# Seven products of a slab pair in another order, diagonal copies on ScalarE, first loads on ScalarE's queue, last sums first

## The chip, the cores and the metric

One core of a Trainium2 chip. The metric is the device time of one execution in microseconds (us), as the median of the runs shown; lower is better.

## The reference, cut to what matters

One inference step of a diffusion backbone with a single trunk layer, on 128 context tokens and 512 latent tokens together (640 columns), model width 1024, in float32:

```
h = rms_norm(x, norm_pre[0]) * (1 + sc1) + sh1
x = x + 0.5 * g1 * rms_norm(swiglu(h, ffn_w_in[0], ffn_w_out[0]), norm_post[0])
h = rms_norm(x, norm_pre[1]) * (1 + sc2) + sh2
m, s_f, s_b = mixer(h, ...)        # Fourier mixing and a two-way HGRN2 scan of 4 heads
x = x + g2 * rms_norm(m, norm_post[1])
h = rms_norm(x, norm_pre[2]) * (1 + sc3) + sh3
x = x + 0.5 * g3 * rms_norm(swiglu(h, ffn_w_in[1], ffn_w_out[1]), norm_post[2])
```

where `swiglu(h) = (silu(h @ Wg) * (h @ Wu)) @ Wout` with 2816 hidden columns, and the shifts, scales and gates come from `silu(cond) @ w_mod + b_mod`.

## The kernel before, in words

Every large product is made of three passes over a split of both operands into a high part (a rounding copy, `_hi`, made by ScalarE) and a low part (the remainder, `_lo`, made by GpSimd or VectorE by a subtraction): hi*hi, hi*lo and lo*hi. Weights are streamed as slabs of 128 columns. SyncE loads a slab when `slab_done` says that its buffer is free, ScalarE makes its high part (`next_hi`, L1201 to L1208), GpSimd its low part (L550), TensorE multiplies. Each engine has its program written out by hand, in order, and waits on semaphores, so an instruction behind a waiting one waits too.

**Front.** SyncE issues eight small loads (identity, vectors) and then five tiles of x, two slabs of `w_mod`, three weight slabs and two more slabs of `w_mod` (L413 to L434). TensorE transposes the vectors, runs 52 idle transposes (`keep_busy`), and transposes the five normalized tiles. ScalarE squares and scales the tiles (L1229, L1235). Then come two products with `w_mod` (`early_mod`), whose row ScalarE copies out (`mod_rows`, L1246) before it makes the first high parts; TensorE folds the row; VectorE makes the modulation vectors (L1700, L1710) and the first h (L1717, L1732); `first_slab` (L827) multiplies the first three slabs step by step, as h comes. GpSimd makes the low parts of those slabs in six halves (`FIRST_LO`).

**Heads.** While TensorE runs the four slabs of head h, it also runs the seven levels of the scan of head h-1. At each level VectorE scales queries and keys (`scale_queries` with L1975 to L1992, `scale_keys` L1959 and L1960), ScalarE copies keys (`level_keys`, L1466), and TensorE runs the level's small products (L951). At level 6 VectorE also copies the 32x32 blocks of ATN onto the diagonal of AT (four copies, L1991), between four copies beside the diagonal (L1992). After level 7's keys TensorE transposes the keys (`keys_to_tokens`, L656).

**Seven products.** For 18 of the 22 slab pairs of the second FFN, a gate slab and a value slab are multiplied by Strassen's scheme, with seven products of half size and sums on VectorE. One product (`product`, L1145) is 12 matmuls of 320 columns. Per pair p there are four result banks x, y, z, v, and seven products in this order: (1) x from the gate's first half; (2) y from s2; (3) x again from the gate's second half, added to the bank; (4) y again from the value's first half, added; (5) z from s1; (6) v from the value's second half; (7) z again from s4, added. Before (3), ScalarE has to copy x out to A_P1 (`p1_copied`, L1644). VectorE then makes U2 = P1 + y after (2) (L2261), U3 = P1 + y after (4) (L2269), C22 = U3 + z after (5) (L2274), C21 after (6) (L2281), the first half of the hidden tile (L2284), C12 after (7) (L2223), and the second half (L2228). Between these it makes the sums s1, s2 and a difference (L2190 to L2195) and s4 (L2204) of the next pair, and two low parts of it (`lows`, L2213 and L2216). ScalarE applies SiLU to x (L1648) after (3) and to C12 (`second_gate`, L1633), and makes the high parts of the next pair; GpSimd makes five low parts of it (L559). Each engine does this in a fixed order; ScalarE runs `second_gate` of pair p-1, then the copy of x of pair p, and `second_gate` waits for C12.

**Split of the hidden tiles.** After pair 17 the 22 hidden tiles, held whole in M32, are split: ScalarE makes the high part (`whole_high`, L1335), VectorE the low part (`whole_low`, L2233). The last product, out1A and out1B (L631 to L633), starts when the first two tiles are split and its first slab is ready. ScalarE makes that slab's high part in `after_slab` behind the SiLU of x of pair 17.

**Last sums.** When out1A is done, VectorE adds sums of squares (`y_sum`, L1750) and updates x (`x_add`, L1755 and L1757) for three tiles, one tile after the other, and then makes low parts of out1B's slabs 6, 9 and 12 (`slab_low`, L1793). ScalarE runs `y_std` (L1275) of each tile between the high parts of out1B's slabs.

Of the kernel before, what the change touches and what calls it, by code (L numbers as in the profile page):

```python
# [3 lines left out]
P = 128  # L4
# [125 lines left out]
def hybrid_step_kernel(nc, x_prompt, x_sample, state_hgrn, c, c_ctx, w_mod, b_mod, norm_pre, norm_post,  # L130
# [280 lines left out]
    def _(sp):  # L411

        sp.dma_start(ident[:, :], t_const).then_inc(sem("const_in"), 16)  # L413
        sp.dma_start(rowsA[0:72, :], b_mod.rearrange("l (r q) -> (l r) q", q=P)).then_inc(sem("rows_in"), 16)
        sp.dma_start(rowsA[72:96, :], norm_pre.rearrange("l s (r q) -> (l s r) q", q=P)).then_inc(sem("rows_in"), 16)
        sp.dma_start(rowsA[96:120, :], norm_post.rearrange("l s (r q) -> (l s r) q", q=P)).then_inc(sem("rows_in"), 16)
        sp.dma_start(rowsB[0:4, :], hgrn_gain.rearrange("l (r q) -> (l r) q", q=P)).then_inc(sem("rows_in"), 16)
        sp.dma_start(rowsB[4:20, :], lb_logits.rearrange("l d (r q) -> (l d r) q", q=P)).then_inc(sem("rows_in"), 16)
        sp.dma_start(rowsB[20:28, :], c.rearrange("l (r q) -> (l r) q", q=P)).then_inc(sem("rows_in"), 16)
        sp.dma_start(rowsB[28:36, :], c_ctx.rearrange("(r q) -> r q", q=P)).then_inc(sem("rows_in"), 16)  # L420
# [126 lines left out]
    def _(pool):  # L547
# [5 lines left out]
        for i, half in FIRST_LO:  # L553
            pool.wait_ge(hi_done, i + 1)
            if (i, half) == (2, 0):
                pool.wait_ge(sem("h0_ready"), KT // 2)
            subtract(i, 4 * half, 4 * half + 4).then_inc(sem("first_lo"), 1)
# [3 lines left out]
        def seven_low(p):  # L561
# [31 lines left out]
    def _(pe):  # L593
# [111 lines left out]
        keep_busy(52, PP[3][:, 0, 0:P])  # L705
# [265 lines left out]
        def outputs(hd):  # L971

            pe.wait_ge(sem("sv_done"), hd + 1)
# [182 lines left out]
        for p in range(SEVEN):  # L1156
# [26 lines left out]
            if p > 1:  # L1183
                pe.wait_ge(sem("hid_b"), p - 1)
            product(z, s1, T1).then_inc(sem("product"), 1)
            pe.wait_ge(sem("seven_lo"), 5 * p + 4)
# [11 lines left out]
    def _(act):  # L1198
# [22 lines left out]

        act.wait_ge(sem("const_in"), 16)
# [28 lines left out]

        mod_rows(2, modrow[0])
        next_hi()
# [214 lines left out]

        def load_states(hd):
# [92 lines left out]
        for m, (n, pr) in enumerate(((0, 0), (0, 1), (1, 0))):  # L1562
            level_keys(last, 2 * m + 2)
            level_keys(last, 2 * m + 3)
# [31 lines left out]
        def value_highs(p):  # L1596
# [4 lines left out]
            A(s2[0][:, :, :], s2[2][:, :, :], ACT.Copy).then_inc(sem("seven_hi"), 1)  # L1601
            act.wait_ge(sem("s_made"), 4 * p + 3)
# [735 lines left out]
```

## Time and profile before

| what | value |
|---|---|
| median of 3 runs | 1442.42 us (1439.97 to 1444.91) |
| the profiled execution's own time | 1442.57 us |
| its span, first to last instruction | 1440.0 us |
| TensorE busy (matmul) | 1404.4 us, 98% |
| VectorE busy | 722.6 us, 50% |
| ScalarE busy | 527.9 us, 37% |
| GpSimd busy | 658.7 us, 46% |
| mean granted TensorE clock | 0.996 |

The span is shorter than the execution's time by the 2.57 us that lie around it. TensorE's busy time is that of pipelined matmuls, so it says where TensorE waits, and not that it works at its peak.

### The profile page before, as it was taken

What the parts mean: (1) busy time and instruction counts of PE and PEld (TensorE: products, weight loads), DVE (VectorE), ACT (ScalarE), POOL (GpSimd) and SP (SyncE); (2) the same over time, 40 slices, a digit from 0 to 9 for tenths busy, and PEclk for the clock granted to TensorE, in tenths of its full rate; (3) what the DMA queues carried; (4) which work ended last, traced back from release to release, by engine and by line L of the source; (5) the groups of instructions that cost most, each with busy time, mean ns of one, the idle gap of its engine ahead of it and who ended that gap; (6) DMA issues with size and microseconds to landing.
All of it is one profiled execution on the core that took longest, in us unless ns stands there. A gap on an engine that the chain in (4) does not pass through costs nothing.

```text
span 1440.0 us, 23202 instructions
## 1 busy us (share of the span) xinstructions
PE 1404.4 (98%) x9661; PEld 1294.8 (90%) x9661; DVE 722.6 (50%) x1067; ACT 527.9 (37%) x791; POOL 658.7 (46%) x507
## 2 busy tenths in 40 slices
PE   6999999999999999999999999999999999989998
PEld 5899999999888888998989999989999999978876
DVE  3388888211001431478777312144677777766043
ACT  6312222222334663233434222266344334345233
POOL 0333433344566682323223433543455565558663
PEclk9999999999999999999999999999999999999999
DMA  9766664222545551212112222413122232235465
GB/s 320 267 211 214 203 235 133 67 80 76 174 129 164 175 198 47 61 52 61 51 40 64 74 73 74 146 59 103 45 74 80 82 88 74 74 89 159 132 184 181
DMA packets 215291, 173.32 MB, mean 120 GB/s; under 512 B 6472, under 2 KB 175636, under 8 KB 215060
## 3 DMA queue, kind: packets, MB, share of 16 engines
q1 hardware_dynamic: 212820, 170.78, 37.7%
q8 instruction: 76, 1.25, 0.3%
q10 hardware_dynamic: 2368, 1.07, 0.3%
q14 instruction: 27, 0.22, 0.1%
HBM read 168.65 MB, written 3.17 MB: 119 GB/s over the span
## 4 chain that ended last, share of the span: by engine, by line
PE 82%; DVE 9%; issue 4%; ACT 2%; DMA 1%; SPq 1%; POOL 0%; DVEq 0%; ACTq 0%
PE PP L612 42%; PE PP L631 8%; PE PP L633 8%; PE PP L632 8%; PE PP L1145 7%; DVE W_lo L2216 2%; DVE S_in L2204 2%; PE PP L656 1%; PE PP L827 1%; PE PP L670 1%; PE PP L951 1%; DMA XTOK<-in_x_sample 1%; DVE TT L2223 1%; PE PP L967 1%; DMA W_in<-in_ffn_w_out 1%
## 5 line engine op out<-in xcount | busy, mean ns | idle before, releaser
L550 POOL TENSOR_TENSOR W_lo<-W_in,W_hi 128x512 fp32r<-128x512 f32 (+1 forms) x380 | 481.0, 1291 | 645.7 <-ACT W_hi L1208 639.1
L1208 ACT ACTIVATE W_hi<-W_in 128x1024 fp32r<-128x1024 f32 x181 | 190.9, 1057 | 445.6 <-PE PP L612 262.5
L612 PE MATMUL PP<-Hhi,W_hi 128*128 128x320 f32 (+2 forms) x1216 | 285.9, 313 | 0.0
L612 PE MATMUL PP<-Hlo,W_hi 128*128 128x320 f32 (+2 forms) x1216 | 280.9, 309 | 0.0
L612 PE MATMUL PP<-Hhi,W_lo 128*128 128x320 f32 (+2 forms) x1216 | 280.8, 309 | 0.0
L612 PEld LDWEIGHTS PP<-Hhi,W_hi 128*128 128x128 f32 x1216 | 202.6, 188 | 9.0 <-issue 6.9
L612 PEld LDWEIGHTS PP<-Hhi,W_lo 128*128 128x128 f32 x1216 | 204.4, 188 | 0.0
L612 PEld LDWEIGHTS PP<-Hlo,W_hi 128*128 128x128 f32 x1216 | 204.4, 188 | 0.0
L559 POOL TENSOR_TENSOR W_lo<-W_in,W_hi 128x512 fp32r<-128x512 f32 x54 | 77.7, 1453 | 99.1 <-DVE W_in L2195 93.0
L1877 DVE SCALAR_TENSOR_TENSOR PP<-modl,S,PP 128x512 f32<-128x512 f32 x144 | 95.8, 744 | 0.0
L631 PE MATMUL PP<-W_hi,Mlo 128*128 128x512 f32 x220 | 86.8, 395 | 4.8 <-DVE Mhi L2233 3.2
L631 PE MATMUL PP<-W_hi,Mhi 128*128 128x512 f32 x220 | 86.3, 392 | 0.8 <-POOL W_lo L550 0.3
L633 PE MATMUL PP<-W_hi,Mhi 128*128 128x512 f32 x220 | 86.3, 392 | 0.0
L632 PE MATMUL PP<-W_lo,Mlo 128*128 128x512 f32 x220 | 86.2, 392 | 0.0
L632 PE MATMUL PP<-W_lo,Mhi 128*128 128x512 f32 x220 | 85.7, 389 | 0.0
L633 PE MATMUL PP<-W_hi,Mlo 128*128 128x512 f32 x220 | 85.6, 389 | 0.0
L1793 DVE TENSOR_TENSOR W_lo<-W_in,W_hi 128x1024 fp32r<-128x1024 f32 x13 | 18.8, 1443 | 115.8 <-ACT W_hi L1208 115.8
L1145 PE MATMUL PP<-Hhi,W_hi 128*128 128x320 f32 x216 | 67.9, 315 | 7.6 <-ACT TT L1644 7.6
L1856 DVE TENSOR_TENSOR TT<-TT,PP 128x640 f32<-128x640 f32 x22 | 18.1, 822 | 108.9 <-PE PP L612 106.8
L1145 PE MATMUL PP<-Hlo,W_hi 128*128 128x320 f32 x216 | 66.8, 309 | 0.0
L1145 PE MATMUL PP<-Hhi,W_lo 128*128 128x320 f32 x216 | 66.7, 309 | 0.0
L631 PEld LDWEIGHTS PP<-W_hi,Mlo 128*128 128x128 f32 x220 | 41.6, 189 | 15.2 <-DVE Mhi L2233 3.5
(294 smaller groups left out, 2682.6 us busy)
## 6 DMA issues: line engine op xcount, KB each, us to landing
W_in<-in_ffn_w_out SPq DMA_DIRECT2D x176, 256.0 KB, 3.1
W_in<-in_ffn_w_in SPq DMA_DIRECT2D x83, 512.0 KB, 3.9
modl<-in_w_mod SPq DMA_DIRECT2D x14, 2048.0 KB, 9.2
W_in<-in_w_in SPq DMA_DIRECT2D x32, 512.0 KB, 3.9
modw<-in_w_mod SPq DMA_DIRECT2D x4, 2048.0 KB, 14.2
HL<-g_rows SPq DMA_DIRECT2D x6, 512.0 KB, 5.7
V_in<-in_w_in SPq DMA_DIRECT2D x10, 256.0 KB, 3.6
O_in<-in_w_out SPq DMA_DIRECT2D x10, 256.0 KB, 6.0
```

Source lines behind the costliest of these rows:

```text
L550: return nc.gpsimd.tensor_tensor(lo[:, k0:k1, :], full[:, k0:k1, :], hi[:, k0:k1, :].bitcast(fp32), ALU.subtract)
L559: return nc.gpsimd.tensor_tensor(lo, full, hi.bitcast(fp32), ALU.subtract)
L612: m = mm(out[:, 0:c1 - c0], w[:, k, :], src[:, c0:c1], start=lead and n == 0 and a == 0, stop=tail and n == len(x) - 1 and a == 2)
L631: mm(out, xh, wh, start=lead and kk == 0, stop=False)
L632: mm(out, xh, wl, start=False, stop=False)
L633: m = mm(out, xl, wh, start=False, stop=tail and kk == 1)
L1145: m = mm(out, wk[:, k, :], xk[:, k, :], start=not add and k == 0 and a == 0, stop=k == KH - 1 and a == 2, skip_group_check=add)
L1208: A(W[i][0], W[i][2], ACT.Copy).then_inc(hi_done, 1)
L1793: V.tensor_tensor(lo, full, hi.bitcast(fp32), ALU.subtract).then_inc(sem("lo_dve"), 1)
L1877: m = V.scalar_tensor_tensor(acc if k < KT - 1 else mod_set(i)[cnd][:, :], w, weight, acc, ALU.mult, ALU.add)
L2204: V.tensor_tensor(s4[2][:, :, :], gate[2][:, KH:KT, :], s2[2][:, :, :], ALU.subtract)\
L2216: V.tensor_tensor(lo, full, hi.bitcast(fp32), ALU.subtract).then_inc(sem("seven_lo_dve"), 1)
```

## The change

Five parts. (a) The eight small loads move from SyncE's queue to ScalarE's, ahead of all else there; the copies of the vectors move behind the first two squares; `keep_busy` has 56 transposes in place of 52; the first slab's high part is made ahead of the copy of the modulation row; GpSimd's low part of the second slab waits for the first finished h. (b) ScalarE makes the four diagonal copies of each head, between the key copies of levels 6 and 7. (c) The order of the seven products is x, y, z, y again, x again, v, z again; GpSimd's and ScalarE's parts of the next pair follow that order, s4 is made before U3, and the SiLU of x comes behind the next pair's high parts. (d) In the last pair the first four hidden tiles are split beside the products. (e) The three `y_sum` come first, then `slab_low` and `x_add` in turn.

```diff
@@ SyncE, and at the head of ScalarE's program with act in place of sp
-        sp.dma_start(ident[:, :], t_const).then_inc(sem("const_in"), 16)
-        sp.dma_start(rowsA[0:72, :], b_mod.rearrange(...)).then_inc(sem("rows_in"), 16)
...
@@ GpSimd
-            if (i, half) == (2, 0):
-                pool.wait_ge(sem("h0_ready"), KT // 2)
+            if half == 0 and i:
+                pool.wait_ge(sem("h0_ready"), (1, KT // 2)[i - 1])
...
+            low(*(x[:, :, :] for x in s1)).then_inc(sem("seven_lo"), 1)
+            pool.wait_ge(sem("seven_hi"), 7 * p + 5)
             low(*(x[:, 0:KH, :] for x in value)).then_inc(sem("seven_lo"), 1)
-            pool.wait_ge(sem("seven_hi"), 7 * p + 5)
-            low(*(x[:, :, :] for x in s1)).then_inc(sem("seven_lo"), 1)
@@ TensorE
-        keep_busy(52, PP[3][:, 0, 0:P])
+        keep_busy(56, PP[3][:, 0, 0:P])
...
         def outputs(hd):
+            pe.wait_ge(sem("at_diagonal"), hd + 1)
...
             product(y, s2, T2).then_inc(sem("product"), 1)
-            pe.wait_ge(sem("seven_lo_dve"), 2 * p + 2)
-            pe.wait_ge(sem("p1_copied"), p + 1)
-            product(x, part(gate, KH, KT), b21, True).then_inc(slab_done, 1)
             pe.wait_ge(sem("seven_lo"), 5 * p + 2)
+            if p == 0:
+                pe.wait_ge(sem("t_lo"), 2)
+            if p > 1:
+                pe.wait_ge(sem("hid_b"), p - 1)
+            product(z, s1, T1).then_inc(sem("product"), 1)
+            pe.wait_ge(sem("seven_lo"), 5 * p + 3)
             pe.wait_ge(sem("u2_done"), p + 1)
...
             product(y, part(value, 0, KH), T3, True).then_inc(sem("product"), 1)
-            pe.wait_ge(sem("seven_lo"), 5 * p + 3)
...
-            product(z, s1, T1).then_inc(sem("product"), 1)
+            pe.wait_ge(sem("seven_lo_dve"), 2 * p + 2)
+            pe.wait_ge(sem("p1_copied"), p + 1)
+            product(x, part(gate, KH, KT), b21, True).then_inc(slab_done, 1)
             pe.wait_ge(sem("seven_lo"), 5 * p + 4)
...
             product(v, part(value, KH, KT), T4).then_inc(slab_done, 1)
@@ ScalarE
-        act.wait_ge(sem("vec_T"), 2)
-        A(VA[:, :], PP[2][:, 0, 0:120], ACT.Copy).then_inc(sem("vec_evac"), 1)
-        A(VB[:, :], PP[2][:, 1, 0:36], ACT.Copy).then_inc(sem("vec_evac"), 1)
         for t in range(NCH):
+            if t == 2:
+                act.wait_ge(sem("vec_T"), 2)
+                A(VA[:, :], PP[2][:, 0, 0:120], ACT.Copy).then_inc(sem("vec_evac"), 1)
+                A(VB[:, :], PP[2][:, 1, 0:36], ACT.Copy).then_inc(sem("vec_evac"), 1)
             act.wait_ge(sem(f"x_in{t}"), 16)
...
+        next_hi()
         mod_rows(2, modrow[0])
-        next_hi()
         next_hi()
...
+        def diagonal_blocks(hd):
+            act.wait_ge(sem("at_done"), 7 * hd + 5)
+            if hd:
+                act.wait_ge(sem("o_mm"), hd)
+            tiles = AT[:, :].rearrange("p (a b) -> p a b", a=NCH)
+            for q in range(4):
+                part = slice(32 * q, 32 * q + 32)
+                m = A(tiles[part, :, part], ATN[part, :, :], ACT.Copy)
+            m.then_inc(sem("at_diagonal"), 1)
...
                     level_keys(h - 1, 2 * m + 2)
+                    if m == 2:
+                        diagonal_blocks(h - 1)
                     level_keys(h - 1, 2 * m + 3)
...
             if p + 1 < SEVEN:
                 gate_highs(p + 1)
+                value_highs(p + 1)
+            else:
+                for j in range(EARLY_PAIRS):
+                    whole_high(j)
             act.wait_ge(slab_done, i + 1)
             A(x, x, ACT.Silu).then_inc(sem("gate_a"), 1)
-            if p + 1 < SEVEN:
-                value_highs(p + 1)
...
-        for j in range(EARLY_PAIRS):
-            whole_high(j)
         second_gate(SEVEN - 1)
@@ VectorE
                 for t in GROUP[0]:
                     y_sum(2, t)
+                for t in GROUP[0]:
+                    slab_low("out1B", (6, 9, 12)[t])
                     x_add(2, t)
-                for m in (6, 9, 12):
-                    slab_low("out1B", m)
...
                 for q in range(4):
-                    V.tensor_copy(tiles[part, :, part], ATN[part, :, :])
                     m = V.tensor_copy(tiles[part, :, other], near(pair_of(hd, lev))[part, :, :])
...
                 first_sums(p + 1)
-            dve.wait_ge(sem("product"), 5 * p + 3)
+                last_sum(p + 1)
+            else:
+                whole_low(0)
+            dve.wait_ge(sem("product"), 5 * p + 4)
...
             V.tensor_tensor(A_U3, A_P1, y, ALU.add).then_inc(sem("u3_done"), 1)
-            dve.wait_ge(sem("product"), 5 * p + 4)
...
             V.tensor_tensor(A_C22, A_U3, z, ALU.add).then_inc(sem("c22_done"), 1)
             if p + 1 < SEVEN:
-                last_sum(p + 1)
                 lows(p + 1)
+            else:
+                whole_low(1)
+                whole_low(2)
...
-        for j in range(EARLY_PAIRS):
+        for j in range(3, EARLY_PAIRS):
             whole_low(j)
```

## Rows read from the trace of the kernel before

**Rows 1.** The page's first part: busy us (share of the span), instructions.

```profile
PE 1404.4 (98%) x9661; PEld 1294.8 (90%) x9661; DVE 722.6 (50%) x1067; ACT 527.9 (37%) x791; POOL 658.7 (46%) x507
```

**Rows 2.** Waits of TensorE, whole span: waiting line, releaser, us, times, longest.

```profile
PE PP L1145 <- ACT TT L1644: 7.6, 17, 0.8
...
PE PP L656 <- DVE KD L1960: 3.3, 3, 1.1
PE PP L631 <- DVE Mhi L2233: 3.2, 1, 3.2
```

**Rows 3.** Timeline of TensorE, one slab pair: start us, us, instruction, idle before.

```profile
1098.93 0.39 PE L1145 MATMUL PP<-Hhi,W_hi 128*128 128x320 f32 x1 [0.41 <-ACT TT L1644]
...
1111.17 0.31 PE L1145 MATMUL PP<-T_hi,S_lo 128*128 128x320 f32 x1
1111.89 0.39 PE L1145 MATMUL PP<-Hhi,W_hi 128*128 128x320 f32 x1 [0.41 <-ACT TT L1644]
```

**Rows 4.** Timelines of VectorE and ScalarE in the same pair.

```profile
1111.78 0.49 DVE L2261 TENSOR_TENSOR TT<-TT,PP 128x320 f32<-128x320 f32 x1 [0.86 <-ACT TT L1644]
...
1111.33 0.42 ACT L1644 ACTIVATE TT<-PP 128x320 f32<-128x320 f32 x1
```

**Rows 5.** The page's DMA issues: count, KB each, us to landing.

```profile
W_in<-in_ffn_w_in SPq DMA_DIRECT2D x83, 512.0 KB, 3.9
```

**Rows 6.** Timelines of TensorE, ScalarE and GpSimd around the end of pair 17.

```profile
1280.38 0.50 PE L631 MATMUL PP<-W_hi,Mlo 128*128 128x512 f32 x1 [3.24 <-DVE Mhi L2233]
...
1270.14 0.42 ACT L1648 ACTIVATE PP<-PP 128x320 f32<-128x320 f32 x1 [2.17 <-PE PP L1145]
...
1271.60 2.56 POOL L550 TENSOR_TENSOR W_lo<-W_in,W_hi 128x512 fp32r<-128x512 f32 x2 [6.48 <-ACT W_hi L1208]
```

**Rows 7.** Window around it: us, busy of each engine, granted clock, DMA.

```profile
1268.00:1290.00 22.00, 18.65 (x95) 16.60 (x96) 10.88 (x15) 11.42 (x16) 8.11 (x6) 0.92 0.33 96
```

**Rows 8.** Timeline of one head: VectorE from level 5 to level 7, then ScalarE.

```profile
674.89 0.33 DVE L1986 COPY_PREDICATED ATN<-near_mask,PP 128x160 f32<-128x160 uint8 x1
...
678.01 0.30 DVE L1991 COPY AT<-ATN 32x160 f32<-32x160 f32 x1
...
680.55 0.49 DVE L1959 TENSOR_TENSOR KD<-KD,FD 128x320 f32<-128x320 f32 x1
...
676.36 0.74 ACT L1466 ACTIVATE KX<-KD 128x640 f32<-128x640 f32 x1 [3.58 <-DVE KD L1960]
```

**Rows 9.** Timeline of the front: SyncE's issues, ScalarE, VectorE.

```profile
0.74 0.40 SPq L413 DMA_DIRECT2D ident<-in_t_const  x1
...
3.82 0.36 SPq L421 DMA_DIRECT2D XTOK<-in_x_prompt  x1
...
10.24 14.52 SPq L434 DMA_DIRECT2D W_in<-in_ffn_w_in  x3
...
14.00 1.06 ACT L1229 ACTIVATE YB<-XTOK 128x1024 f32<-128x1024 f32 x1
...
27.66 0.60 ACT L1246 ACTIVATE modrow<-PP 128x512 f32<-128x512 f32 x1 [3.56 <-PE PP L670]
...
28.15 2.00 ACT L1208 ACTIVATE W_hi<-W_in 128x1024 fp32r<-128x1024 f32 x2
...
29.90 1.91 DVE L1710 SCALAR_TENSOR_TENSOR Avec<-MV,VA 128x4 f32<-128x4 f32 x2
...
47.59 0.36 DVE L1710 SCALAR_TENSOR_TENSOR Avec<-MV,VA 128x4 f32<-128x4 f32 x2
```

**Rows 10.** DMA issues from 9.9 to 11 us: count, KB, us from issue to landing.

```profile
W_in<-in_ffn_w_in SPq DMA_DIRECT2D x1, 512.0 KB, 16.4
```

**Rows 11.** Timeline of ScalarE in the heads: two DMA issues on its own queue.

```profile
640.20 0.83 ACTq L1489 DMA_DIRECT2D out<-SO  x2
```

**Rows 12.** Waits of TensorE from 1300 to 1440 us.

```profile
PE PP L631 <- POOL W_lo L550: 1.2, 2, 0.8
PE PP L631 <- DVE W_lo L1793: 0.3, 1, 0.3
```

More of the change, by code:

```diff
@@ L411, in _ @@
     def _(sp):
-        sp.dma_start(ident[:, :], t_const).then_inc(sem("const_in"), 16)
[L414 to L420, printed above, removed]
         sp.dma_start(XTOK[:, 0, :], x_prompt[0]).then_inc(sem("x_in0"), 16)
@@ L1179, in _ @@
             product(y, part(value, 0, KH), T3, True).then_inc(sem("product"), 1)
-            pe.wait_ge(sem("seven_lo"), 5 * p + 3)
+            pe.wait_ge(sem("seven_lo_dve"), 2 * p + 2)
+            pe.wait_ge(sem("p1_copied"), p + 1)
+            product(x, part(gate, KH, KT), b21, True).then_inc(slab_done, 1)
+            pe.wait_ge(sem("seven_lo"), 5 * p + 4)
             if p == 0:
                 pe.wait_ge(sem("t_lo"), 3)
-            if p > 1:
-                pe.wait_ge(sem("hid_b"), p - 1)
-            product(z, s1, T1).then_inc(sem("product"), 1)
-            pe.wait_ge(sem("seven_lo"), 5 * p + 4)
             if p > 1:
@@ L1219, in root_table @@
             A(spare[:, n:n + 1], ident[:, 0:1], ACT.Sqrt)
+        act.dma_start(ident[:, :], t_const).then_inc(sem("const_in"), 16)
+        act.dma_start(rowsA[0:72, :], b_mod.rearrange("l (r q) -> (l r) q", q=P)).then_inc(sem("rows_in"), 16)
+        act.dma_start(rowsA[72:96, :], norm_pre.rearrange("l s (r q) -> (l s r) q", q=P)).then_inc(sem("rows_in"), 16)
+        act.dma_start(rowsA[96:120, :], norm_post.rearrange("l s (r q) -> (l s r) q", q=P)).then_inc(sem("rows_in"), 16)
+        act.dma_start(rowsB[0:4, :], hgrn_gain.rearrange("l (r q) -> (l r) q", q=P)).then_inc(sem("rows_in"), 16)
+        act.dma_start(rowsB[4:20, :], lb_logits.rearrange("l d (r q) -> (l d r) q", q=P)).then_inc(sem("rows_in"), 16)
+        act.dma_start(rowsB[20:28, :], c.rearrange("l (r q) -> (l r) q", q=P)).then_inc(sem("rows_in"), 16)
+        act.dma_start(rowsB[28:36, :], c_ctx.rearrange("(r q) -> r q", q=P)).then_inc(sem("rows_in"), 16)
         act.wait_ge(sem("const_in"), 16)
         root_table(0)
-        act.wait_ge(sem("vec_T"), 2)
-        A(VA[:, :], PP[2][:, 0, 0:120], ACT.Copy).then_inc(sem("vec_evac"), 1)
-        A(VB[:, :], PP[2][:, 1, 0:36], ACT.Copy).then_inc(sem("vec_evac"), 1)
         for t in range(NCH):
+            if t == 2:
+                act.wait_ge(sem("vec_T"), 2)
+                A(VA[:, :], PP[2][:, 0, 0:120], ACT.Copy).then_inc(sem("vec_evac"), 1)
+                A(VB[:, :], PP[2][:, 1, 0:36], ACT.Copy).then_inc(sem("vec_evac"), 1)
             act.wait_ge(sem(f"x_in{t}"), 16)
@@ L1563, in _ @@
             level_keys(last, 2 * m + 2)
+            if m == 2:
+                diagonal_blocks(last)
             level_keys(last, 2 * m + 3)
@@ L1601, in value_highs @@
             A(s2[0][:, :, :], s2[2][:, :, :], ACT.Copy).then_inc(sem("seven_hi"), 1)
+            A(s1[0][:, :, :], s1[2][:, :, :], ACT.Copy).then_inc(sem("seven_hi"), 1)
             act.wait_ge(sem("s_made"), 4 * p + 3)
             A(value[0][:, 0:KH, :], value[2][:, 0:KH, :], ACT.Copy).then_inc(sem("seven_hi"), 1)
-            A(s1[0][:, :, :], s1[2][:, :, :], ACT.Copy).then_inc(sem("seven_hi"), 1)
             act.wait_ge(raw_full[BUF[i + 1]], NEED[i + 1])
@@ L1619, in _ @@
                 if (grp, j) == (1, 0):
-                    for c, (hi, _, whole) in enumerate((T2, T1, T4)):
+                    for hi, _, whole in (T2, T1, T4):
                         act.wait_ge(sem("t_made"), 4)
@@ L2201, in last_sum @@
             if p:
-                dve.wait_ge(sem("product"), 5 * (p - 1) + 4)
+                dve.wait_ge(sem("product"), 5 * (p - 1) + 3)
             dve.wait_ge(sem("s_made"), 4 * p + 2)
```

## The prediction

> **What bounds the kernel now.** I read the page first: TensorE is busy for 98% of the span [rows 1], VectorE for half. So only time in which TensorE stands still can be won, some 36 us in all. The second view is the table of TensorE's waits [rows 2]. The reader sees there that three names carry most of it: 17 waits of the seven products for ScalarE's copy of x, 3 waits in the heads for the keys of level 7, and one wait ahead of the last product. The third view is the timeline of one slab pair [rows 3, 4], where the wait repeats; the fourth and fifth are the timeline and the window around the end of the pairs [rows 6, 7]; then the heads [rows 8], the front [rows 9 to 11] and the waits of the last product [rows 12].
>
> **Part c, the order of the seven products.** Per pair the idle time is read start to start: 0.72 us between the last matmul ahead of the wait and the first behind it, against 0.147 for a running one ((1111.17 - 1098.93) / 83), so 0.57 lost, and the first matmul takes 0.39 in place of 0.31 [rows 3]. That is 0.65 a pair, and 17 pairs wait [rows 2]: 11.0 us. One period is 1111.89 - 1098.93 = 12.96 us, while 84 matmuls by 0.147 need 12.3. Why is it 12.96? It is a loop: product (3) of a pair waits for the copy of x, that for SiLU of C12 on ScalarE, that for C12 on VectorE, which stands behind C21, the two lows and s4, and those behind C22, which needs product (5) of the pair before. So the loop holds three products, (3), (4) and (5), 3 x 12 x 0.147 = 5.3 us, and 12.96 - 5.3 = 7.7 us of VectorE, ScalarE and signalling.
>
> After the change x is added fifth, with two more products ahead of it, so the copy of x is 3.5 us less urgent. What becomes urgent is U2: product (4) still needs it. Product (1) starts at 1111.17 + 0.15 - 3.52 = 1107.80; U2 ended at 1111.78 + 0.49 = 1112.27 [rows 4], 4.5 us later, and the new product (4) starts 3 x 1.76 = 5.3 us after (1). So even if nothing came earlier, U2 would be 0.8 us in time. The new loop holds one product, (4), with U3 behind it: 1.8 + 7.7, without s4 (it now waits for product (3) and goes ahead of U3) and with U2 and U3 at 0.5 each: some 9.5 us, under the 12.3 that TensorE needs. The five highs of the next pair go ahead of SiLU of x; they have no hurry, since x comes two products later. The gate slab's buffer is now freed by the fifth product in place of the third, 3.5 us later; its load takes 3.9 us [rows 5] and the slab is multiplied only two pairs later, 24 us, so ScalarE and VectorE find it some 2 us before they need it. SyncE's queue holds nothing else there. I cost these moves at nothing; without that cover a late load would stall the highs, and TensorE some 4 us after that. I take 11.0; the ends are 5 (U2 late by some 0.3 in each pair) and 11.7 (pair 0 and longer pairs too).
>
> **Part d, the end of the pairs.** TensorE idles 3.24 us [rows 6], and then the granted clock falls: over 22 us it is 0.92 [rows 7], which is 0.08 x 22 = 1.8 us at full speed, the lower level (1.2 GHz) for some 3.5 us. Lost: 5.0. Tiles 0 to 3 are split during pair 17: four highs on ScalarE behind the copy of x, three lows on VectorE behind sums that pair 18 would have needed, so in free time. What is late next is the first slab of the last product: its high part stands behind SiLU of x on ScalarE. Before, SiLU began at 1270.14 and the low part was done at 1271.60 + 2.56 = 1274.16 [rows 6], 4.0 us behind product (3) and its SiLU. SiLU now comes behind the fifth product, and two products, 3.5 us, are left: so 4.0 - 3.5, and 0.2 for the signal to SiLU (an estimate), 0.7 us of idle time remain, up to 1.2 if VectorE's lows slow GpSimd. I assume that so short a wait costs no clock. Gain 5.0 - 1.0 = 4.0, between 2.5 and 4.6.
>
> **Part b, the heads.** Eight copies lie between 678.01 and 680.55 [rows 8], 0.32 each; half of them go, 1.27 us, right ahead of level 7's keys, for which TensorE waits 1.1 us three times, 3.3 in all [rows 2]. ScalarE's four copies can begin when level 5's predicated copy ends, 674.89 + 0.33 = 675.22, in the 3.58 us of idle time before the key copy at 676.36 [rows 8]. The trace shows no such copy on ScalarE: at VectorE's 0.32 four take 1.3 and end at 676.5, 0.1 late; at 0.74, what the whole key copy takes, they end 1.8 late, which would delay the keys of level 7 by 0.6 or so, as VectorE reaches them 1.27 earlier. I take the first, for its size is the nearer. The fourth head waits for nothing there and gains nothing. Gain 3.3, between 1.5 and 3.5.
>
> **Part a, the front.** SyncE issued x's first load at 3.82; now at 0.74: every load behind it, w_mod and weights too, comes 3.1 us earlier, less 0.4 (an estimate) for sharing the engines with 0.16 MB of small loads that used to run alone. ScalarE now issues those: two took 0.83 us [rows 11], so eight take 3.3, until 4.1, and its first square waits for x anyway. What then sets the modulation row is the first slab's load, since its high part now stands ahead of the row's copy: landed at 10.24 + 16.4 = 26.6 before [rows 9, 10], now at 23.9; with 1.0 for the high part (two took 2.00) the row's copy starts at 24.9 in place of 27.66 [rows 9]: 2.8 won. The two Avec instructions took 1.91 us while GpSimd made low parts, and 0.36 in the second round without it [rows 9]. The first low part is now over by then and the second waits: 1.55 won. But that second low part (one half, 1.28, like those of rows 6) starts with the first h, and TensorE has only six matmuls, 0.9 us, of the other slab: 0.4 lost. The four more idle transposes fall into a pause. Sum 3.9, between 0 and 5.
>
> The Trainium skill ("DMA: Bandwidth & Descriptors", section "Issuing engines are not separate DMA queues") says that issuing from a second engine saves only the issuing time, as all loads share the same DMA engines. By that alone the front would win at most those 3.1 us and the whole sum would be 0.8 smaller; the Avec term is no matter of loads, so I keep my sum.
>
> **Part e.** In the last product TensorE waits 1.5 us in three places for low parts of slabs 4 to 6 [rows 12]. ScalarE's high parts stand behind `y_std`, which waits for a `y_sum` that stood behind an `x_add`. With the sums first, slabs 5 and 6 are in time; slab 4's is behind the first sum as before, and its GpSimd half only loses the contention. Gain 1.1, between 0.4 and 2.
>
> **Sum.** 11.0 + 4.0 + 3.3 + 3.9 + 1.1 = 23.3. The profiled execution took 1442.57 us, 0.15 over the median 1442.42, so 1442.57 - 23.3 = 1419.3, and 1419 for the median.
>
> **Rivals.**
> - **The stall moves to U2.** If U2 is late, product (4) waits in each pair. For it: U2 has only 0.8 to 1 us to spare. Against: C12 comes sooner, as it no longer stands behind s4. At 0.3 us a pair 5 to 6 us are lost: 1425.
> - **Small loads land behind x.** The vectors are awaited at the third square. If the small loads queue behind the five tiles, they land with the last of them, at 14.0 - 3.1 = 11 [rows 9]; with transposes and copies three squares of 1.06 and their sums remain, and the row is 1 us later than before in place of 2.8 earlier. The front then wins nothing: 1423. No row shows two queues loaded at once. The Trainium skill (the same page, "Queues, rings and completion order") says that a DMA engine serves the queues in turns, packet by packet; by that the small loads land about as before and this rival falls.
> - **Slower: VectorE's loop becomes the bound.** Place: lows, C21, C12 and U2 of one pair, with GpSimd beside them. The other parts win 12.3 us, so the pairs would have to lose those: 12.3 / 18 = 0.7 a pair above 12.96, a loop of 13.7. That decides if the new loop, some 9.5, grows by more than 4 us, as if both lows took over twice as long. At a loop of 14 it gives 1442.4 + 6 = 1448. Nothing in the trace speaks for it.
> - **Nothing gained.** Every wait is replaced by another just behind it: 1440 to 1442.
>
> **How the numbers follow.** Forecast 0.72, U2 0.10, small loads 0.12, slower 0.02, nothing 0.04. About 0.3%, 4.3 us, is what a measurement here can tell from no change. The forecast's own range is 1414 to 1424, from the ends of its terms; with the first two rivals and a scatter of 2.5 us in the runs shown the range is 1414 to 1426. Faster by over 0.3%: 0.94; within: 0.04; slower: 0.02.
>
> **What would show it.** Right: no waits of L1145 for ScalarE and a period of 12.3 us; the first matmul of the last product within 1.2 us of the last of pair 17, and a full granted clock behind it; no wait for the keys of level 7; the row's copy near 25 us and the first product of slab 0 near 30; fewer waits for low parts in out1B. Wrong: waits of L1145 for VectorE's U2 (L2261 before), a row's copy at 27 or later, ScalarE's key copy of level 7 much later than VectorE's keys, or a half clock anywhere in the last 180 us.

## The result, and the profile after

The changed kernel takes 1417.79 us (median of four runs, 1416.67 to 1420.16) beside 1441.52 for the kernel before: a ratio of 0.9834, with a 95% interval from 0.9812 to 0.9857. The forecast was 1419.0 and its range 1414 to 1426. The profiled execution took 1420.16 us, the longest of the four.

The page's first part and TensorE's waits over the whole span, of the changed kernel:

```profile
PE 1396.2 (98%) x9665; PEld 1292.1 (91%) x9665; DVE 695.2 (49%) x1051; ACT 534.0 (38%) x807; POOL 661.0 (47%) x507
```

```profile
PE PP L648 <- DMA rowsB<-in_c_ctx: 9.7, 1, 9.7
PE PP L648 <- ACT YB L1291: 2.2, 1, 2.2
PE PP L819 <- DVE Hlo L1751: 1.5, 4, 0.7
PE PP L623 <- POOL W_lo L542: 1.0, 2, 0.7
```

All three names of [rows 2] are gone: the 17 waits for the copy of x, the three for the keys of level 7, and the one for the last low parts. So are the waits for low parts in the last product [rows 12]; what the fourth line has left there is 0.66 us ahead of out1A. Two lines are new or longer: the first small rows of the program, and 2.2 us for a normed tile in out0 (the last product of the first FFN). Neither is in the sum of the prediction, and both are the subject of experiments below. In the kernel before, TensorE's timeline has these two waits in the front, which [rows 2] doesn't show, one ahead of the 52 idle transposes and one behind them:

```profile
4.94 0.43 PE L656 MATMUL PP<-ident,rowsA 120*128 120x120 f32 x1 [4.94 <-DMA rowsB<-in_c_ctx]
...
16.84 7.18 PE L656 MATMUL PP<-ident,YB 128*128 128x128 f32 x40 [3.96 <-ACT YB L1235]
```

VectorE's timeline of one slab pair (C12 is L2241, U2 L2279), which answers to [rows 4]:

```profile
1102.10 0.49 DVE L2241 TENSOR_TENSOR TT<-TT,PP 128x320 f32<-128x320 f32 x1 [0.68 <-PE PP L1138]
1105.68 0.49 DVE L2279 TENSOR_TENSOR TT<-TT,PP 128x320 f32<-128x320 f32 x1 [3.09 <-PE PP L1138]
...
1114.42 0.49 DVE L2241 TENSOR_TENSOR TT<-TT,PP 128x320 f32<-128x320 f32 x1 [0.67 <-PE PP L1138]
```

The period is 1114.42 - 1102.10 = 12.32 us, what 84 matmuls need, in place of 12.96. Both sums now wait for TensorE: VectorE stood idle for 3.09 us ahead of U2. The end of the pairs answers to [rows 6, 7]: TensorE's first matmul of out1A, and the window behind it with the granted clock in the third column from the end.

```profile
1262.88 0.47 PE L623 MATMUL PP<-W_hi,Mlo 128*128 128x512 f32 x1 [0.66 <-POOL W_lo L542]
```

```profile
1262.00:1284.00 22.00, 21.34 (x95) 17.39 (x94) 18.37 (x13) 14.82 (x20) 18.88 (x13) 1.00 0.52 157
```

In the heads ScalarE's four diagonal copies and the key copy behind them [rows 8]:

```profile
674.13 1.38 ACT L1481 ACTIVATE AT<-ATN 32x160 f32<-32x160 f32 x4 [2.47 <-DVE ATN L2005]
675.54 0.74 ACT L1470 ACTIVATE KX<-KD 128x640 f32<-128x640 f32 x1
```

The copies take 0.35 us each, close to VectorE's 0.32, and with the key copy right behind them they fit into the idle time, as the prediction chose to assume. The front, which answers to [rows 9], in TensorE's, ScalarE's and VectorE's timelines:

```profile
9.69 0.43 PE L648 MATMUL PP<-ident,rowsA 120*128 120x120 f32 x1 [9.69 <-DMA rowsB<-in_c_ctx]
10.05 0.32 PE L648 MATMUL PP<-ident,rowsB 36*128 36x36 f32 x1
10.30 8.32 PE L648 MATMUL PP<-ident 128*128 128x128 f32 x56
18.46 4.64 PE L648 MATMUL PP<-ident,YB 128*128 128x128 f32 x40
...
31.96 0.53 PE L819 MATMUL PP<-Hhi,W_hi 128*128 128x320 f32 x2 [0.19 <-DVE Hlo L1751]
...
4.12 0.36 ACTq L1224 DMA_DIRECT2D rowsB<-in_c_ctx  x1
...
23.14 1.06 ACT L1203 ACTIVATE W_hi<-W_in 128x1024 fp32r<-128x1024 f32 x1 [0.31 <-DMA W_in<-in_ffn_w_in]
26.73 0.60 ACT L1250 ACTIVATE modrow<-PP 128x512 f32<-128x512 f32 x1 [2.53 <-PE PP L662]
...
28.98 0.36 DVE L1729 SCALAR_TENSOR_TENSOR Avec<-MV,VA 128x4 f32<-128x4 f32 x2
```

Avec takes 0.36 us as foreseen, and the first slab's high part starts at 23.14, when its load has landed. But the row's copy stands at 26.73 and waits for TensorE, whose 56 idle transposes ran until 18.6, behind rows that came only at 9.69.

One table carries the rest. It has, for the profiled execution of each kernel named in this document, where the first slab, the first level of the heads and the seven products start, where the span ends, and the three lengths between (us, from the lines' first instructions):

```
kernel        slab   heads  seven   end     to heads  to seven  to end
before        34.4   606.9  1043.6  1440.0  572.5     436.7     396.4
changed       32.0   607.1  1040.3  1418.4  575.1     433.2     378.1
changed again 31.8   605.0  1037.6  1415.7  573.2     432.6     378.1
diag_only     31.9   605.4  1037.9  1434.4  573.4     432.5     396.5
undo_sums     31.6   604.7  1037.5  1415.5  573.2     432.7     378.0
undo_split    31.4   606.6  1039.1  1423.2  575.2     432.5     384.1
loop5_before  32.3   608.9  1045.6  1488.7  576.6     436.7     443.1
loop5_after   32.5   609.6  1042.5  1422.9  577.2     432.9     380.4
loop12_after  31.2   606.8  1039.4  1506.5  575.6     432.6     467.1
idle32        30.0   607.4  1040.4  1418.5  577.3     433.0     378.1
loads_sync    33.7   608.5  1041.2  1419.3  574.9     432.7     378.1
front_order   29.4   605.0  1037.7  1415.9  575.6     432.8     378.2
sum_scalar    32.0   604.8  1037.3  1415.4  572.8     432.5     378.1
best          29.2   603.9  1036.4  1414.5  574.7     432.5     378.1
```

The last two lengths repeat within 0.7 us wherever the code is the same. The first column and the first length do not: they differ by up to 2.5 and 5 us between executions of the same code, about as much as the runs themselves. The first length has three levels. It is 572.5 to 573.4 in the five traces in which TensorE doesn't wait for the normed tile in out0 (before, changed again, diag_only, undo_sums, sum_scalar). It is 574.7 to 575.6 where it waits there for 1.6 to 2.3 us. And it is 576.6 to 577.3 in loop5_before, loop5_after and idle32, where the granted clock is also down behind that wait. The window behind it, in the changed kernel and in idle32 (clock in the third column from the end):

```profile
530.00:560.00 30.00, 27.76 (x130) 22.60 (x129) 7.82 (x15) 14.01 (x25) 2.56 (x2) 1.00 0.02 6
```

```profile
530.00:560.00 30.00, 27.75 (x123) 22.67 (x122) 6.57 (x13) 13.82 (x25) 2.52 (x2) 0.94 0.02 5
```

For the first two rows of the table: 1.8 us are won up to the start of in0 (the slabs of the first FFN behind the first three), 2.0 are lost from there to the heads, 3.5 are won in the heads and 18.3 behind them, in sum the 21.6 by which the span is shorter. The 2.0 are out0's wait, which the profiled execution of the changed kernel has and that of the kernel before has not.

### The profile page after: what moved, and what is told of

Its sections match the earlier page's. It is cut to its first block, busy times and chain, and to the rows that moved or that the text cites. A ratio compares the mean times of both kernels' runs of the same rounds, so it can differ in the third digit from the quotient of the medians.

```text
span 1418.4 us, 23218 instructions
## 1 busy us (share of the span) xinstructions
PE 1396.2 (98%) x9665; PEld 1292.1 (91%) x9665; DVE 695.2 (49%) x1051; ACT 534.0 (38%) x807; POOL 661.0 (47%) x507
## 4 chain that ended last, share of the span: by engine, by line
PE 95%; DVE 2%; ACT 1%; POOL 0%; issue 0%; DMA 0%; ACTq 0%; DVEq 0%; POOLq 0%
PE PP L604 45%; PE PP L1138 15%; PE PP L623 9%; PE PP L625 9%; PE PP L624 9%; PE PP L648 2%; PE PP L819 1%; PE PP L943 1%; PE PP L662 1%; DVE ST L1769 1%; PE PP L959 1%; POOL W_lo L542 0%; PE PP L837 0%; PE PP L1013 0%; DMA rowsB<-in_c_ctx 0%
## 5 line engine op out<-in xcount | busy, mean ns | idle before, releaser
L551 POOL TENSOR_TENSOR W_lo<-W_in,W_hi 128x512 fp32r<-128x512 f32 x54 | 84.9, 1586 | 82.2 <-ACT S_hi L1620 80.2
L1812 DVE TENSOR_TENSOR W_lo<-W_in,W_hi 128x1024 fp32r<-128x1024 f32 x13 | 15.9, 1225 | 119.5 <-ACT W_hi L1203 119.5
L551 POOL TENSOR_TENSOR S_lo<-S_in,S_hi 128x512 fp32r<-128x512 f32 x36 | 54.4, 1510 | 0.0
```

Source lines behind the costliest of these rows:

```text
L551: return nc.gpsimd.tensor_tensor(lo, full, hi.bitcast(fp32), ALU.subtract)
L1812: V.tensor_tensor(lo, full, hi.bitcast(fp32), ALU.subtract).then_inc(sem("lo_dve"), 1)
```

## The experiments

### Is it a loop, and how much slack has it now?

In each pair the sum C12 is made six (or thirteen) times in place of once, one after the other on VectorE; the result is the same. One repeat measured 0.52 us.

```
+            for _ in range(5):      # 12 in the third kernel
+                link(V.tensor_tensor(A_C12, A_U2, seven_banks(p)[2], ALU.add))
             V.tensor_tensor(A_C12, A_U2, seven_banks(p)[2], ALU.add).then_inc(sem("c12_done"), 1)
```

Kernel before, five repeats:

> The kernel before, with the sum C12 made six times in place of once in every pair of the seven products, one after the other on VectorE (the result is the same). One such sum takes 0.41 us in the trace, with its signal some 0.5, so C12 is ready some 2.5 us later. Theory (a loop through products (3) to (5), C12, SiLU and the copy of x sets the period of 12.96): every pair is 2.5 us longer, 17 pairs, +42 us, between +34 and +50. Rival (the wait is one for an engine with time to spare: VectorE is busy for half of the span): under +5 us.

Changed kernel, five repeats:

> The changed kernel with the same five repeats. Theory (the new loop holds one product and is some 3 us shorter than the 12.3 that TensorE needs): hidden, 0 to +5 us. Rival (U2 has only the 0.8 to 1 us to spare that the prediction gave it, and C12 is on its way): 1.5 us a pair, +26 us.

Changed kernel, twelve repeats:

> The changed kernel with twelve repeats, C12 some 6 us later. Theory (slack of some 3 us, then the loop bounds again): about 3 us a pair, +50 us, between +35 and +60, and product (4) waits for U2. Rival (C12 is no longer on any loop): under +5 us.

Measured, one run each beside 1440.95 for the kernel before: 1490.53, 1424.97 and 1508.34 us. TensorE's wait for the copy of x in the first of them, and its wait for U2 in the third:

```profile
PE PP L1145 <- ACT TT L1644: 39.2, 17, 3.1
```

```profile
PE PP L1138 <- DVE TT L2281: 51.1, 17, 3.1
```

The kernel before pays for every repeat, though VectorE is half idle: it was a loop. Of the +49.6, 46.7 lie behind the start of the pairs (443.1 in place of 396.4), 2.7 a pair for repeats of 2.6; the rest lies ahead of them, where this execution has out0's wait and the lower clock behind it. In the changed kernel five repeats leave no wait in the pairs at all, and the clock stays full; the window of the pairs in that kernel:

```profile
1042.00:1264.00 222.00, 222.00 (x1516) 222.00 (x1516) 187.60 (x317) 88.58 (x178) 133.21 (x89) 1.00 0.28 81
```

The 2.3 us that it needs more behind the start of the pairs lie in the last product: SiLU of pair 17's C12, five repeats later, stands ahead of the high parts of the next slabs on ScalarE, and TensorE waits 2.06 us for a low part made from one of them. Of the +7 beside the changed kernel's median, above the +5 that was expected at most, the repeats explain these 2.3; the first length is 577.2, with out0's wait and the fall of the clock. So the rival by which U2 is short of time falls. With twelve repeats the wait is the 3 us per pair that the theory gave, but the time is +90 beside the changed kernel's median where +50 was expected. Most of the rest is the clock, in the window of the pairs, and 5.7 us are a wait for a low part in the last product:

```profile
PE PP L623 <- POOL W_lo L542: 6.7, 3, 5.7
```

```profile
1040.00:1344.00 304.00, 252.22 (x1513) 247.89 (x1512) 259.86 (x437) 90.74 (x179) 133.12 (x89) 0.90 0.21 61
```

0.10 x 304 = 30 us at full speed are lost to the lower level (1.2 GHz) behind the waits of 3.0 us. In the kernel before a wait of 0.4 us in every pair cost no clock: it is 1.00 from 1044 to 1277.

What the new loop consists of shows in the same trace: VectorE is idle for 0.34 us until product (7) releases C12, then SiLU, the copy of P1 and U2 follow, and then products (4) to (7). The period there is 17.10 us; less 6.23 for the repeats and 1.6 for the lower clock in products (4) to (7), which take 8.65 in place of 48 x 0.147 = 7.06, that is 9.3. The prediction's figure was 9.5, but for a loop that went through one product, (4), and then VectorE's U3, lows and C21. That path ends 0.34 us earlier here, and 0.68 in the pair of the changed kernel shown above, for C12 waits for TensorE in both. So the loop goes through four products and not through one: the length was right by luck, and the path was not.

### The heads alone

On the kernel before, only the diagonal copies move:

```
+        def diagonal_blocks(hd):
+            act.wait_ge(sem("at_done"), 7 * hd + 5)
...
+                m = A(tiles[part, :, part], ATN[part, :, :], ACT.Copy)
...
-                    V.tensor_copy(tiles[part, :, part], ATN[part, :, :])
```

> The kernel before with ScalarE's copy of half of the diagonal alone. Prediction: no wait of TensorE for the keys of level 7, 3.3 us off the heads; by the milestones of the changed kernel 3.7: from the first level of the heads to the start of the seven products 433.0 to 433.4 in place of 436.7. Rival (ScalarE's copies end late and hold back its keys): 434 to 436. The time 2.7 to 4 us below the kernel before, if out0 does not hide it by its own wait of 2.2 us.

Measured: 1435.42 us beside 1439.42, ratio 0.9967 (0.9956 to 0.9977), and 432.5 in place of 436.7 us from the heads to the seven products: 4.2 won, a little more than expected, no wait for keys left, and nothing taken back by ScalarE.

### The end of the pairs and the last product

The splits of tiles 0 to 3 behind the last pair again, ScalarE's high parts and VectorE's low parts:

```
-            else:
-                for j in range(EARLY_PAIRS):
-                    whole_high(j)
             act.wait_ge(slab_done, i + 1)
...
+        for j in range(EARLY_PAIRS):
+            whole_high(j)
         second_gate(SEVEN - 1)
...
-            else:
-                whole_low(0)
...
-            else:
-                whole_low(1)
-                whole_low(2)
...
-        for j in range(3, EARLY_PAIRS):
+        for j in range(EARLY_PAIRS):
             whole_low(j)
```

> The changed kernel with tiles 0 to 3 split behind the last pair again. Theory of the prediction: the last product starts 3.2 us after the last of pair 17 in place of 0.7, and the granted clock falls behind it: +4.0 us, between 2.5 and 4.6. Rival (with products six and seven behind x, the splits end early enough without being moved): under +1 us.

The low parts of the last product behind the sums and `x_add` again:

```
                 for t in GROUP[0]:
                     y_sum(2, t)
-                for t in GROUP[0]:
-                    slab_low("out1B", (6, 9, 12)[t])
                     x_add(2, t)
+                for m in (6, 9, 12):
+                    slab_low("out1B", m)
```

> The changed kernel with the low parts of slabs 6, 9 and 12 behind the three sums with x_add, as before. Prediction: +1.1 us, between 0.4 and 2, with waits for low parts of slabs 4 to 6 in the last product. From the stretches of the traces (the last product and its surroundings were 2.5 us shorter than the other terms explain): +2.5. From the start of the seven products to the end of the span 379.2 or 380.6 in place of 378.1. Rival (the sums were hidden, and the earlier end of the splits freed the low parts): within 0.5.

Measured: 1424.82 (1423.93 to 1425.06) and 1417.54 us (1416.34 to 1421.83). In the traces the stretch to the end is 6.0 us longer without part d, more than the 4.6 expected at most, and 0.1 shorter without part e. The first matmul of out1A without part d:

```profile
1266.21 0.79 PE L623 MATMUL PP<-W_hi,Mlo 128*128 128x512 f32 x1 [5.15 <-DVE Mhi L2250]
```

It waits longer than in the kernel before, 5.15 against 3.24 us, since SiLU of x now comes behind the fifth product, and the high splits stand behind the high parts of two slabs that follow it. The second of these waits itself, 2.31 us for its load, in ScalarE's timeline of that kernel:

```profile
1261.26 1.06 ACT L1203 ACTIVATE W_hi<-W_in 128x1024 fp32r<-128x1024 f32 x1 [2.31 <-DMA W_in<-in_ffn_w_out]
1262.22 2.60 ACT L1339 ACTIVATE Mlo<-M 128x640 fp32r<-128x640 f32 x4
```

The clock falls as well, to 0.92 in the 22 us around it. So part c made part d dearer to leave out. And part e is worth nothing here: without it the last product has no wait for a low part either. The three waits of [rows 12] were those of one execution: of the two other traces with the old order and the old splits, diag_only has one such wait, of 0.5 us, and loop5_before one, of 1.3.

### The front

Three kernels: 32 idle transposes in place of 56; the small loads back on SyncE's queue, ahead of x; and an order in which TensorE doesn't wait for the rows before it starts to idle. The third also moves ScalarE's two copies of the vectors behind the last square, and VectorE's reciprocal ahead of the bounds, so it is not an experiment on the idle transposes alone; of its edit only TensorE's part is shown.

```
-        keep_busy(56, PP[3][:, 0, 0:P])
+        keep_busy(32, PP[3][:, 0, 0:P])
```

> The changed kernel with 32 in place of 56 idle transposes ahead of those of x. Theory (the idle transposes, 8.3 us, hold up the transposes of x, for whose input they were still running in the changed kernel's trace): the transposes of x start some 3 us earlier, or as soon as x is normed, and the modulation row's copy stands near 25 in place of 26.7; the first slab starts 1 to 1.7 us earlier, the same TensorE clock. Rival (the load of the first slab's weights sets the row, as the prediction said): 0, the row's copy stays within 0.3 us of 26.7.

```
+            sp.dma_start(ident[:, :], t_const).then_inc(sem("const_in"), 16)
...
             sp.dma_start(XTOK[:, 0, :], x_prompt[0]).then_inc(sem("x_in0"), 16)
```

> The changed kernel with the eight small loads back at the head of SyncE's queue, as in the kernel before. Theory (the small rows land near 5 again, x some 3 us later than in the changed kernel, and W0 and w_mod too): row's copy at 25.5 to 27.7, first slab at 32 to 34, that is 0 to 2 us later than the 31.2 to 32.5 of the changed kernel's three traces. Rival (the early issue is worth nothing, as the rows were late by as much): first slab within 0.5 us of those.

```
-        pe.wait_ge(sem("rows_in"), 16 * 7)
-        transpose(PP[2][:, 0, 0:120], rowsA[:, :]).then_inc(sem("vec_T"), 1)
-        transpose(PP[2][:, 1, 0:36], rowsB[:, :]).then_inc(sem("vec_T"), 1)
...
-        keep_busy(56, PP[3][:, 0, 0:P])
+        keep_busy(30, PP[3][:, 0, 0:P])
+        pe.wait_ge(sem("rows_in"), 16 * 7)
+        transpose(PP[2][:, 0, 0:120], rowsA[:, :]).then_inc(sem("vec_T"), 1)
+        transpose(PP[2][:, 1, 0:36], rowsB[:, :]).then_inc(sem("vec_T"), 1)
+        keep_busy(24, PP[3][:, 0, 0:P])
...
```

> The changed kernel with 30 idle transposes ahead of the wait for the small rows and 24 behind, ScalarE's two copies of the vectors behind the last square, and VectorE's reciprocal ahead of the bounds. Theory (small rows that land late, and idle transposes queued behind them, hold up the transposes of x): row's copy near 24.5 in place of 26.7, first slab at 29.5 to 30 in place of 31.2 to 32.5, 2 us off the time unless out0 takes them again, 1414.5 to 1417.5. Rival (the loads of W0 and w_mod set the row): the row's copy at 26 or later.

Measured: row's copy at 24.81, 27.24 and 24.15, first slab at 30.0, 33.7 and 29.4; times 1420.31, 1421.62 (one run each) and 1417.94 (1417.64 to 1418.78), the last a little above its range. The transposes in the kernel with 32:

```profile
9.96 5.47 PE L648 MATMUL PP<-ident 128*128 128x128 f32 x32
15.26 5.23 PE L648 MATMUL PP<-ident,YB 128*128 128x128 f32 x40
```

The transposes of x start 3.2 us earlier, so the idle ones stood on the path, and the load of the first slab (W0) did not set the row. With the loads on SyncE it does, as ScalarE's timeline of that kernel shows:

```profile
26.28 1.06 ACT L1211 ACTIVATE W_hi<-W_in 128x1024 fp32r<-128x1024 f32 x1 [3.59 <-DMA W_in<-in_ffn_w_in]
27.24 0.58 ACT L1250 ACTIVATE modrow<-PP 128x512 f32<-128x512 f32 x1
```

With the new order it does too, as the prediction had it, and 3.1 us earlier:

```profile
23.19 1.06 ACT L1204 ACTIVATE W_hi<-W_in 128x1024 fp32r<-128x1024 f32 x1 [2.58 <-DMA W_in<-in_ffn_w_in]
24.15 0.58 ACT L1250 ACTIVATE modrow<-PP 128x512 f32<-128x512 f32 x1
```

The two front orders win 2.0 and 2.6 us at the first slab, but the kernel with 32 is at the heads as late as the changed kernel. Both wait in out0 for 2.2 us; the kernel with 32 also has the lower clock behind that wait, 0.06 x 30 = 1.8 us in the window shown above.

### The wait in out0

VectorE's timeline in out0 of the changed kernel, GpSimd's beside it, and TensorE behind them:

```profile
519.54 9.82 DVE L1769 TENSOR_TENSOR ST<-ST 128x1 f32<-128x1 f32 x2
529.56 0.16 DVE L1774 RECIPROCAL ST<-ST 128x1 f32<-128x1 f32 x1 [0.20 <-ACT ST L1279]
...
526.75 2.53 POOL L542 TENSOR_TENSOR V_lo<-V_in,V_hi 128x512 fp32r<-128x512 f32 x2
534.86 2.56 POOL L542 TENSOR_TENSOR V_lo<-V_in,V_hi 128x512 fp32r<-128x512 f32 x2 [5.59 <-ACT V_hi L1203]
...
533.89 1.09 PE L648 MATMUL PP<-ident,YB 128*128 128x128 f32 x8 [2.24 <-ACT YB L1291]
```

Two sums of one column take 9.82 us; in the last product three of them take 0.28. GpSimd makes low parts without a pause from 509.1 until 529.28; the first of the two sums takes 9.75 us and ends then. The experiment makes the sum on ScalarE and takes VectorE's out:

```
+            act.wait_ge(sem("y_ss"), y_seq(b, t, 1) + 1)
+            A(ST[:, 2, t:t + 1], ST[:, 0, t:t + 1], ACT.Identity, bias=ST[:, 1, t:t + 1]).then_inc(sem("y_sum"), 1)
             act.wait_ge(sem("y_sum"), b * NCH + t + 1)
...
-            V.tensor_tensor(ST[:, 2, t:t + 1], ST[:, 0, t:t + 1], ST[:, 1, t:t + 1], ALU.add)\
-                .then_inc(sem("y_sum"), 1)
...
```

> The changed kernel with the one-column sum of the norm made on ScalarE in place of VectorE (the same numbers are computed). In five of six traces so far, of the kernel before with repeats among them, one such sum on VectorE took some 9.8 us in out0 beside GpSimd's low parts, and TensorE then waited 2.24 us for the normed tile, in two of them with a fall of the granted clock behind it; from the first slab to the first level of the heads 575.1 to 577.4 us went by, in the one trace without it 572.5. Theory (VectorE's sum is starved while GpSimd runs without a pause): no sum above 0.5 us, no wait of TensorE for that tile, 572.5 (within 0.7) for that stretch, and a time of 1413 to 1415.5. Rival (the sum is only the last to come: the squares' statistics or the load of the tile are as late): the wait stays above 1.5 us, and the time within 1 us of 1417.8.

Then both edits together, with the changed kernel run again on the same chip:

> The reordered front and the sum on ScalarE together, on the changed kernel. Theory (the two waits are independent: the first slab at 29.4 with the one, 572.8 us from there to the heads with the other, 810.7 from the heads' start to the span's end in the changed kernel's trace, so a span near 1413 and a profiled time near 1414.7): median 1414 to 1416.5, and 2 to 4 us below the changed kernel run again beside it. Rival (each of the two alone left the median at 1417.9 and 1418.9, so what they win in the trace is lost elsewhere in most executions): within 1 us of the changed kernel run again.

> The changed kernel unchanged, on the same chip as the others of this set. Theory (its front varies by 1 to 2 us with the landing of the first loads, and the one-column sum in out0 is starved in most executions): 1416.5 to 1420.5, first slab between 31 and 32.7, TensorE's wait of 2.2 us in out0 there again. Rival (the starved sum was an accident of that execution): no such wait.

Measured: 1418.95 (1417.24 to 1419.57), 1416.53 (1414.61 to 1416.57) and 1420.61 us (1417.52 to 1421.94). With the sum on ScalarE the wait is gone from the trace and the stretch to the heads is 572.8, as the theory says; but the time is above the theory's range, 1417.24 in the profiled execution too, since its front was at 32.0. The trace of both edits together tells why that is possible, in VectorE's and GpSimd's timelines:

```profile
519.59 8.25 DVE L1776 SCALAR_TENSOR_TENSOR XTOK<-YB,ST,XTOK 128x1024 f32<-128x1024 f32 x1
527.76 0.15 DVE L1774 RECIPROCAL ST<-ST 128x1 f32<-128x1 f32 x1
...
524.21 2.54 POOL L542 TENSOR_TENSOR V_lo<-V_in,V_hi 128x512 fp32r<-128x512 f32 x2
531.65 2.56 POOL L542 TENSOR_TENSOR V_lo<-V_in,V_hi 128x512 fp32r<-128x512 f32 x2 [4.90 <-ACT V_hi L1204]
```

Now `x_add`, 1.28 us behind the long sums of the changed kernel, takes 8.25, and TensorE waits 1.55 us. So it isn't the sum as such: it can be the next VectorE instruction with two inputs in SBUF that stands there while GpSimd has no pause. And it comes and goes: of twelve traces with the sum on VectorE eight have the long sum (one of the three with the front and out0 of the kernel before), and the changed kernel run again does not, against the theory's expectation. So it is neither the change's doing nor undone for good by this edit.

The two edits together are the fastest kernel of the study: 4.1 us below the changed kernel run beside it, with no run of the one among the runs of the other. But undo_sums, whose trace has the same waits of TensorE as that of the changed kernel run again, has a median of 1417.54 on this chip and a run of 1416.34, so the edits may be worth 1 us or 4. Against the kernel before the ratio of the two together is 0.9837 (0.9823 to 0.985), and the changed kernel's own was 0.9834 in its first runs and 0.9865 (0.985 to 0.988) on this chip, so across the sets of runs the two are not told apart.

## Why the prediction was right, point by point

The total was right within 1.2 us, and what parts b, c and d remove was named rightly; but the front was over-estimated and the rest under-estimated, and that the two nearly cancel is luck. So is the last microsecond: against 23.3 predicted the medians differ by 23.7 us, and by 18.8 where both kernels were run again (1439.42 and 1420.61). The range of 1414 to 1424 is a judgement and not the sum of the terms' ends, as the prediction has it: these add up to gains of 9.4 and 26.8, that is 1433 and 1416.

- **Part c.** 11.0 predicted; the seven products take 221.6 us from the first to the last matmul in place of 233.2: 11.6. The period, the missing waits and U2 in time are as said. U2 itself ends 1.0 us ahead of product (4) (1106.17 and 1107.18), close to the 0.8 foreseen, but what it waits for is TensorE's product (2) and no longer the chain behind C12. That chain has far more to spare: VectorE idles 3.09 us ahead of U2, and five repeats, 2.6 us, cost the pairs nothing. The step that failed is "The new loop holds one product", which the twelve repeats show to be four.
- **Part b.** 3.3 predicted, 3.5 to 4.2 measured in the pairs of traces. The mis-sized term is the wait itself. In part c the prediction read the loss from start to start and found 0.65 us where the view of waits says 0.41; in parts b, d and e it took the view's figure. The same 0.24 on each of three waits gives 3 x 1.34 = 4.0; start to start, a wait of 1.10 us in the heads lost 1.32.
- **Parts d and e.** 4.0 + 1.1 predicted. The stretch from the seven products to the end is 18.3 shorter, and less 11.6 for part c 6.7 are left: 3.24 - 0.66 of idle time and 1.8 of clock (the idle time left was foreseen as 0.7, and the clock is full, as said), and for the three waits of [rows 12] their 1.5 and again 3 x 0.24. The step that failed is part e: the waits of [rows 12] went, but not by the reordered sums, since undoing these brings none back. What removed them was not tried apart; they differ between executions of the old order, and neither undo_split nor undo_sums has any.
- **Part a.** 3.9 predicted, 1.8 in the pair of traces (in0 starts at 62.5 in place of 64.2), and less on the whole: in the three traces with the old front in0 starts at 62.7 on average, in the seven with the new one at 62.3. The profiled execution of the kernel before happened to have the latest first slab of the three: its last tile of x landed at 13.98, against 12.52 and 12.87 in diag_only and loop5_before, which have the same front. So two figures that the sum starts from were those of one execution. The row's copy, 27.66 there, stands at 25.43 and 25.79 in the other two, earlier than the 25.95 to 27.25 of the seven traces with the new front; and the two Avec, 1.91 us there, take 0.9. On the average the row won nothing. The step that failed is "What then sets the modulation row is the first slab's load". The load came when it was expected (23.14 against 23.9), but the small rows came at 9.69, and "the four more idle transposes fall into a pause" was wrong with all 56 of them: they ended at 18.6, while x was ready to be transposed at 15.5, and the row waited for them. The pause was the 3.96 us shown above; with x earlier and the rows later there was none. Without the idle transposes in the way, in front_order, W0's load sets the row at 24.15, near the 24.9 foreseen.
- **The rivals.** The rival on small loads came true by half: the last rows landed 5.6 us after their issue (4.12 to 9.69), where 1.5 us were enough ahead of the large loads (3.48 to 4.94 in the kernel before); they were not behind all of x, whose fourth and fifth tiles landed at 9.34 and 10.39, but late enough to bind by way of the idle transposes. The Trainium skill's sentence that the queues are served in turns, packet by packet ("DMA: Bandwidth & Descriptors", "Queues, rings and completion order") fits with the rows not being last; the prediction's conclusion, that they would land about as before, is not borne out. The Trainium skill's rule that a second issuing engine wins only the issuing time (the same page, "Issuing engines are not separate DMA queues") fits: W0's high part starts 3.1 us earlier in the changed kernel than with all loads on SyncE (23.14 and 26.28), and the eight issues took SyncE 3.1 us (0.74 to 3.82). The rival of a late U2 and that of a slow VectorE did not occur.
- **The reading of the waits.** "Three names carry most of it" holds only for the lines that [rows 2] shows: these three make 14.1 us of the 36 in which TensorE stood still, and the front's two waits, shown above, another 8.9. The second of them is the pause on which part a counted.

## What to carry to other kernels

A stall that recurs with a half-idle engine is a loop until shown otherwise: put repeats of one link into it, before and after, and the slack is read off the time. A wait costs more than its figure in the view of waits, some 0.24 us each here, and waits of 3 us cost clock as well, as did out0's of 2.2 in three of eight traces. And a gain at the start of a program is not a gain until a later milestone has it: several executions of the same kernel should be laid side by side before 2 us there are put down to an edit, or taken as the start of a sum.

## What was not expected of the hardware

A VectorE instruction with two inputs in SBUF was held up for 8.2 to 9.9 us while GpSimd ran some seven instructions of 1.27 us back to back, and went on only at GpSimd's first pause: in each of the eight traces with the long sum it ends 0.02 us behind the last of them. A reciprocal, which has one input, kept to 0.17 us in the same stretch, just ahead of the long `x_add`. In other executions the same two sums took 2.35 us beside the same GpSimd instructions; there the two `x_add` that follow took 2.2 and 2.1 us, and it was two of GpSimd's instructions that took 2.28 in place of 1.28. What tells the two cases apart stays open. The Trainium skill ("SBUF — State Buffer", "Who interferes with whom") names the kind: a VectorE instruction with two SBUF inputs contends with a GpSimd instruction that reads SBUF. The traces agree, and show that the wait isn't bounded by one such instruction.
